# Spreading the sample rows of v with TensorE into PSUM instead of with DMA into SBUF, and one column split for all input projections

## The reference

```python
def retention_recurrent(q, k, v, S0):
    g = jnp.exp(log_gammas())[None, :, None, None]
    def step(S, qkv):
        q_t, k_t, v_t = qkv
        S = g * S + jnp.einsum('bhd,bhe->bhde', k_t, v_t)
        return S, jnp.einsum('bhd,bhde->bhe', q_t, S)
    ...
hp = jnp.concatenate([meta, x_prompt], axis=1)      # 16 + 1024 tokens
...
y_prompt = hp[:, N_META:]                           # outputs of the meta tokens are dropped
```

## Time and profile before

| | |
|---|---|
| Median of 3 executions | 1251.21 us |
| Profiled execution: its time | 1251.21 us |
| Profiled execution: its span, first to last instruction | 1249.4 us |
| PE busy | 1175.6 us (94%) |
| DVE, ACT, POOL busy | 745.8, 414.9, 424.1 us |
| Mean granted clock of PE | 0.976 |

### The profile page before, as it was taken

One profiled execution on the slowest core, in us unless ns is written; L12 is line 12 of the kernel. 1 busy time (PEld: TensorE's weight loads), 2 busy tenths in 40 slices (PEclk: granted clock), 3 DMA queues, 4 the chain that ended last, 5 costly groups with the idle time before them and its releaser, 6 DMA issues.

```text
span 1249.4 us, 21816 instructions
## 1 busy us (share of the span) xinstructions
PE 1175.6 (94%) x8402; PEld 1161.4 (93%) x8402; DVE 745.8 (60%) x1204; ACT 414.9 (33%) x732; POOL 424.1 (34%) x304
## 2 busy tenths in 40 slices
PE   4999999999999995699999999999999999999995
PEld 3899999999998994599999999999999999999995
DVE  5448899944553137865555655565555555656557
ACT  5244444333344245541313131313132323222222
POOL 3056788221122048632222222222222222222216
PEclk8999999999989997799999999999999999999998
DMA  9211111130052224030202011111212121212143
GB/s 301 67 52 51 35 51 52 34 84 30 26 135 77 85 85 153 18 101 18 85 18 77 24 60 40 51 50 40 61 34 67 34 67 34 67 34 67 35 169 137
DMA packets 99654, 84.50 MB, mean 68 GB/s; under 512 B 2706, under 2 KB 89362, under 8 KB 99594
## 3 DMA queue, kind: packets, MB, share of 16 engines
q1 hardware_dynamic: 99266, 82.63, 21.5%
q10 hardware_dynamic: 336, 1.15, 0.3%
HBM read 72.86 MB, written 11.38 MB: 67 GB/s over the span
## 4 chain that ended last, share of the span: by engine, by line
PE 57%; issue 19%; POOL 13%; DVE 4%; DMA 3%; ACT 2%; POOLq 0%; ACTq 0%; DVEq 0%; SPq 0%
PE ps L320 17%; PE ps L322 17%; PE ps L321 17%; POOL act_lo L605 3%; DMA f_raw<-in_w_ffn_in 3%; POOL f_sum L589 2%; POOL f_sum L591 2%; POOL h_ring L617 1%; POOL o_last L649 1%; POOL f_raw L592 1%; ACT w_ring L941 1%; POOL f_raw L597 1%; DVE w_ring L1350 1%; PE ps L1671 1%; DVE x_lo L1344 1%
## 5 line engine op out<-in xcount | busy, mean ns | idle before, releaser
L320 PE MATMUL ps<-x_hi,w_ring 128*128 128x256 f32 (+1 forms) x1232 | 351.4, 285 | 8.1 <-DVE w_ring L1350 5.8
L322 PE MATMUL ps<-x_lo,w_ring 128*128 128x256 f32 (+1 forms) x1232 | 349.7, 284 | 0.0
L321 PE MATMUL ps<-x_hi,w_ring 128*128 128x256 f32 (+1 forms) x1232 | 349.2, 283 | 0.0
L320 PEld LDWEIGHTS ps<-x_hi,w_ring 128*128 128x128 f32 x1232 | 234.7, 190 | 9.0 <-DVE w_ring L1350 7.8
L321 PEld LDWEIGHTS ps<-x_hi,w_ring 128*128 128x128 f32 x1232 | 235.5, 191 | 0.0
L322 PEld LDWEIGHTS ps<-x_lo,w_ring 128*128 128x128 f32 x1232 | 234.8, 191 | 0.0
L320 PE MATMUL ps<-xn_hi,w_hi 128*128 128x350 f32 (+2 forms) x576 | 187.2, 325 | 0.0
L322 PE MATMUL ps<-xn_lo,w_hi 128*128 128x350 f32 (+2 forms) x576 | 185.3, 322 | 0.0
L321 PE MATMUL ps<-xn_hi,w_lo 128*128 128x350 f32 (+2 forms) x576 | 185.1, 321 | 0.0
L320 PE MATMUL ps<-act_hi,fx_hi 128*128 128x344 f32 x528 | 171.0, 324 | 7.2 <-DVE ffn_acc L1471 6.4
L321 PE MATMUL ps<-act_hi,fx_lo 128*128 128x344 f32 x528 | 168.8, 320 | 0.0
(11 more groups left out here) (191 smaller groups left out, 1893.6 us busy)
## 6 DMA issues: line engine op xcount, KB each, us to landing
f_raw<-in_w_ffn_in SPq DMA_DIRECT2D x44, 512.0 KB, 4.1
raw<-in_w_in SPq DMA_DIRECT2D x24, 512.0 KB, 3.8
f_raw<-in_w_ffn_out SPq DMA_DIRECT2D x22, 512.0 KB, 3.3
raw<-in_w_out SPq DMA_DIRECT2D x8, 512.0 KB, 6.5
h_ring<-in_x_prompt SPq DMA_DIRECT2D x8, 512.0 KB, 4.8
h_scratch<-h_ring SPq DMA_DIRECT2D x8, 512.0 KB, 2.8
h_fin<-h_scratch SPq DMA_DIRECT2D x8, 512.0 KB
out<-o_last SPq DMA_DIRECT2D x8, 512.0 KB
```

What stands on the lines that cost most here:

```text
L320: nc.tensor.matmul(out, hi, mhi, start=first, stop=False, skip_group_check=resumes)
L321: nc.tensor.matmul(out, lo, mhi, start=False, stop=False, skip_group_check=resumes)
L322: return nc.tensor.matmul(out, hi, mlo, start=False, stop=last, skip_group_check=resumes)
```

## The change

The rows of v are no longer spread by DMA. `v_spread(b)` on PE multiplies the 8 rows `v_s` (moving, 512 columns, fp32) with column b of the identity, repeated 128 times (stationary, 8 by 128); the result is row b of v on all 128 partitions, in bank 7 of PSUM. DVE reads it from there. The scratch tensor, the buffers `v_rows` and nine DMAs go. Since bank 7 is taken by one more user, four waits are added or moved. Apart from that, q and g are computed for the meta columns also, and `QG_CHUNKS` and `unit_chunks` go.

```diff
-QG_CHUNKS = [(META, 350 - META)] + IN_CHUNKS[1:]
...
-            sp.wait_ge(s_vs, 1)
-            sp.dma_start(v_scr[:, :], v_s[:, :, :].rearrange("p a n -> p (a n)")).then_inc(s_vout, 16)
             sp.wait_ge(s_smc, 2)
             sp.dma_start(conv_prompt[0, 0], last_u).then_inc(s_cpout, 16)
             sp.dma_start(conv_sample[0, :, CW - 2, :], new_u).then_inc(s_csout, 16)
-            sp.wait_ge(s_vout, 16)
-            for b in range(NS):
-                if b < 2:
-                    sp.wait_ge(s_ptap, CW - 1)
-                else:
-                    sp.wait_ge(s_vbd, b - 1)
-                sp.dma_start(v_rows[:, b % 2, :], v_scr[b:b + 1, :].to_broadcast([P, RW])).then_inc(s_vb[b % 2], 16)
             sp.wait_ge(s_vbd, NS)
...
             def state_update(b):
 
-                dve.wait_ge(s_vb[b % 2], 16 * (b // 2 + 1))
+                dve.wait_ge(s_vb, b + 1)
...
-                    ins = v.scalar_tensor_tensor(out=sv, in0=v_rows[:, b % 2, hh * DH:(hh + 1) * DH],
+                    ins = v.scalar_tensor_tensor(out=sv, in0=ps[:, 7, hh * DH:(hh + 1) * DH],
                                                  scalar=kcol[:, hh, b:b + 1], in1=sv, op0=ALU.mult, op1=ALU.add)
...
-            project(2, 3, (s_ab, 24), s_t1, QG_CHUNKS, xn_hi, xn_lo, s_job)
-            project(3, 4, None, s_t1, IN_CHUNKS, xn_hi, xn_lo, s_job, 3 * SLOTS)
+            project(2, 4, (s_ab, 24), s_t1, IN_CHUNKS, xn_hi, xn_lo, s_job)
...
-                r, (c0, n) = j % H, QG_CHUNKS[j // H]
+                r, (c0, n) = j % H, IN_CHUNKS[j // H]
...
+            def v_spread(b):
+
+                if b % 2 == 0:
+                    pe.wait_ge(s_vs, 1)
+                    pe.wait_ge(s_cs, CT * (b // 2 + 1))
+                else:
+                    pe.wait_ge(s_yn, (b + 1) // 2 + 1)
+                mm(ps[:, 7, :], ident[0:NS, b:b + 1].to_broadcast([NS, P]), v_s[:, :, :],
+                   start=True, stop=True).then_inc(s_vb, 1)
+
             def y_tok(n):
...
+                elif n < 5:
+                    pe.wait_ge(s_vbd, 2 * n - 1)
                 else:
                     pe.wait_ge(s_cs, CT * n)
...
             def y_back(n):
                 m = P if n < TILES else NS
                 pe.wait_ge(s_yn, n + 1)
+                if 1 <= n < 5:
+                    pe.wait_ge(s_vbd, 2 * n)
...
+                if 1 <= n < 5:
+                    v_spread(2 * n - 2)
                 pe.wait_ge(s_st, n + 1)
...
                 if n >= 1:
                     o_back(n - 1)
+                if 1 <= n < 5:
+                    v_spread(2 * n - 1)
```

More of the change, by code:

```diff
@@ L166, in build @@
         yn = at("yn", [P, 2, CC], DD + CT * UCOLS * 4)
-        v_rows = at("v_rows", [P, 2, RW], DD + CT * UCOLS * 4 + SEQ * 4)
         small = DD + CT * UCOLS * 4 + 2 * SEQ * 4
@@ L208, in build @@
                              "oT_done", "ret_out", "ret_hi", "ret_lo"))
-        s_kcol, s_sgam, s_vbd = (sem(n) for n in (
-            "k_sample_scaled", "state_decayed", "state_updated"))
-        s_vout, s_vb = sem("v_sample_out"), [sem(f"v_sample_rows{r}") for r in range(2)]
+        s_kcol, s_sgam, s_vb, s_vbd = (sem(n) for n in (
+            "k_sample_scaled", "state_decayed", "v_sample_spread", "state_updated"))
         s_rp, s_cpout, s_csout = sem("ret_prompt_out"), sem("conv_prompt_out"), sem("conv_sample_out")
@@ L249, in build @@
         h_scr = nc.dram_tensor("h_scratch", [T_OUT, D], F32, kind="Internal").ap()
-        v_scr = nc.dram_tensor("v_scratch", [NS, RW], F32, kind="Internal").ap()
         def half_of(t):
@@ L313, in in_bank @@
             return (r % 2) * 3 + c
-        def unit_chunks(un):
-            return QG_CHUNKS if 8 <= un < 8 + H or un >= N_IN - H else IN_CHUNKS
         def three_pass(out, hi, lo, mhi, mlo, first, last, resumes=False):
@@ L520, in _ @@
                 un, c = divmod(j, 3)
-                c0, n = unit_chunks(8 + un)[c]
+                c0, n = IN_CHUNKS[c]
                 dst = (qT if un < H else kT)[:, un % H, c0:c0 + n]
@@ L723, in _ @@
                     kind, r = un % 2, un // 2
-                for c, (c0, n) in enumerate(unit_chunks(un)):
+                for c, (c0, n) in enumerate(IN_CHUNKS):
                     j = 3 * un + c
@@ L753, in g_silu @@
             def g_silu(j):
-                c0, n = QG_CHUNKS[j // H]
+                c0, n = IN_CHUNKS[j // H]
                 act.wait_ge(s_job, 3 * (N_IN - SLOTS) + j + 1)
```

## The result

The changed kernel takes 1263.26 us (median of 4; 1262.57 to 1266.11) against 1251.11 us before (median of 4). The ratio is 1.010, 95% interval 1.0088 to 1.0112: 12.15 us slower. The forecast was 8.3 us slower, 1259.5 us, with a range up to 1262.0. The direction and what bounds the kernel were right. The price of the spreads was too low, and a change in the clock's low stretch came on top.

The account below looks back on a forecast made before the run. The prediction took PE to bound the kernel in the stretches the change touches. It added 1.2 us for wider q and g jobs and 7.1 for the spreads, 8.3 in all, to 1251.2, giving 1259.5 us, range 1256.0 to 1262.0.

Parts of the forecast that it names:

- What bounds the stretch: Projections of q and stage 3 passes: PE is full, so each microsecond added there moves the program by one.
- q and g: Projections: eight jobs grow from 334 to 350 columns, 0.15 us each, 1.2 us in all on PE.
- The spreads on PE: Passes 1 to 4: eight added fp32 products of 512 columns at `kv`'s 0.89 us each, 7.1 us, uncovered.
- the upper end: Bound from above on the spreads' price in passes 1 to 4: 1.15 us each, 9.2 us in all.
- The new waits: Stage 3 passes: waits around spreads and DVE's updates cost nothing, though both margins are under half a microsecond.
- The margin for `y_back`: Pass 2: the odd spread's update on DVE ends 0.44 us before `y_back`, which waits for it.
- The DMAs that go: Eight reads of `v_rows` beside PE, with no engine listed as waiting: removing them brings no gain, no loss.
- The clock rival: Around `sample_o`: the clock's low stretch changes length, giving 1254.6 to 1263.8 us; chance 0.12, half to each side.
- Stalls: Four passes: odd spreads stall PE through `y_norm` or the update behind it, 2 us, 1261.5 us; chance 0.07.
- cheap fp32: Spreads in passes 1 to 4: 512-column fp32 products cost only the lower bound, 3.8 us, total 1256.2; chance 0.06.
- Taken back: From 458 us on: PE's waits there absorb all 8.3 us, so 1251.2 us, not slower; chance 0.03.

Follow-up runs that it names:

- cols_only: The kernel before with only the wider first column range of q and g (350 instead of 334 columns); 1254.81 us, ratio 1.0018.
- four_pieces: The changed kernel with each spread as four products of 128 columns, still 8 rows; 1264.17 us, ratio 1.0097.
- shift11: The kernel before with its first g job done four times instead of once, no spread; 1263.78 us, ratio 1.0096.
- twice: The changed kernel with each spread done two times in a row; 1270.07 us, ratio 1.0153.
- rows128: The changed kernel with `v_s` zero-filled and the spread contracted over 128 rows; 1261.29 us.
- spread_only: The changed kernel with q and g back at 334 columns, leaving only the spreads on PE; 1261.22 us, ratio 1.0073.
- fp32r_334: The changed kernel with each spread as one fp32r product over 128 rows, and q and g back at 334 columns; 1254.16 us, ratio 1.0016.
- rows32: The changed kernel with `v_s` zero-filled and the spread contracted over 32 rows; 1264.85 us, ratio 1.0105.
- fp32r_spread: The changed kernel with each spread as one fp32r product over 128 rows, high and low parts of v stacked; 1256.92 us.
- after_again: The changed kernel run once more, unchanged; 1263.53 us, ratio 1.0094 against the kernel before.
- gmove_before: The kernel before with the last g job moved between the halves of `sample_o`; 1255.27 us, ratio 1.0038.

## Why the prediction was wrong, by its own steps

- **What bounds the stretch** was right: PE stayed full, and new work on it moved the program one to one up to `sample_o`.
- **q and g:** right, 0.15 to 0.17 us a job; 0.94 us for six jobs and 0.34 for two in cols_only.
- **The spreads on PE:** this step failed. It said "I take `kv`'s 0.89, which has the same type and columns", 7.1 us. They cost 1.22 us each, 9.8 us. The core was even a little cheaper (0.86), but each spread stands alone between 128-row work, and going in and out costs 0.18 us each way. The step weighed rows 6 and 7 against each other and called the product with 16 rows "no cheaper". It was in fact dearer, and the same effect: 1.08 against 0.89 us from start to start. The step compared how long the instructions last, 1.15 against 1.06 us, which leaves out the late start of the load at the way in and the slower pair behind. That is also why the upper end built on it, 8 x 1.15 = 9.2 us, was passed: four_pieces shows the same 1.15 in its row and costs 1.25 us. This step alone is 2.7 us of the 3.9 us by which the forecast was too low.
- **The new waits:** right. The margin for `y_back` came out at 0.60 us (forecast 0.44). The update started 0.11 us behind the spread's slot where 0.20 was taken, and the slot was longer. That an update from PSUM would be nearer 281 ns was wrong: the median is 343 ns (340 to 352) against 344 before. So the like instruction L1245 was not alike enough; it has a constant as its scalar, the update one per partition, and whether that is the reason was not tested. The longer time from PSUM by the Trainium skill, "VectorE: DVE Perf Modes", section on the TRN2 errata, is not borne out by these rows either.
- **The DMAs that go:** right. The DMA share of a pass fell from 0.12 to 0.00 and no engine gained.
- **The clock rival** (chance 0.12) came true in part beside the mis-sized step: 1.6 us in the profiled execution, and shift11 shows that it comes without any spread. Its starting point was also a little off: the old low stretch is 10.2 us, not 9.9. It was wrong to treat it as a case of its own with no weight in the middle. Without it the mis-sized spreads alone would have given 1251.1 + 11.0 = 1262.1 us, at the edge of the range.
- **Stalls, cheap fp32:** neither came. **Taken back:** 0.6 us was, at 475 to 492 us, where the prediction said "gives nothing back".

In the sum, columns and spreads are 1.2 + 9.8 = 11.0 us. The medians leave 0.7 to 1.2 us beside that. In the profiled execution it is 1.0 us: 1.6 of the clock less the 0.6 taken back.

Whether the changed kernel pays the clock's share in all executions, or the kernel before escapes it in some, the profiles (two of the changed kernel, one of the kernel before) do not settle; the runs give 11.7 to 12.15 us between medians.

## What to carry to other kernels

Moving a broadcast from idle DMA queues onto a full TensorE costs what it costs there, all of it; look for who waited for the DMAs first, and here nobody did. When a small matmul is put between large ones, price it by the time from the start of what precedes to the start of what follows, with the same number of rows as its neighbours or with two switches added. How long its instructions last, as a row shows it, is not that price. If it has to be there, zero-fill it to the neighbours' rows (here 1.22 to 0.85 us), and better still make it one fp32r pass (0.29 us).

## What the runs showed of the hardware

- A weight load is not pulled ahead of the running matmul where the contraction changes from 128 rows to 8, 16 or 32, or back: with 8 rows about 0.18 us each way, twice per spread, 2.9 us of the 9.8. Between matmuls of the same few rows it is hidden (four_pieces, twice).
- The low stretch of PE's clock around the 64 single-column matmuls took one of three lengths in the profiles of kernels that left `sample_o` whole: 6.8 us (rows128), 10.2 (before, spread_only, fp32r_334) and 13.7 (after, cols_only, four_pieces, twice, rows32, fp32r_spread, shift11, after_again). The time from `sample_o` to the next O goes with it: 13.6, 15.3 and 16.8 us. It changes without a change in the work itself (shift11 against before); what sets it for one execution the runs do not show. The Trainium skill, "TensorE: Matmul & The Clock Gate", section "What's actually happening", has the monitor free-running. The traces agree as far as they go: where only the start of the work moved, the clock fell 2.9 us into `sample_o` (shift11) instead of 4.0 (before).
- The same single-column work with one dense job in its middle had a low stretch of 3.4 us (gmove_before).
